# Two gate SiLUs and a root one chunk later on ScalarE, with other first tiles and last tiles, in a two-layer hybrid decoder

## The reference

```python
def reference(x, ...):
    for layer in range(2):
        h = rmsnorm(x, mix_norm_w[layer])
        if layer == 0:  # q, k, v, p from h @ w_in; window attention next to a trailing-mean mixer
            x = x + attn_pool_mixer(h, ...)
        else:           # z, xBC, dt from h @ w_in
            x = x + ssd_mixer(h, ...)
        h = rmsnorm(x, ffn_norm_w[layer])
        x = x + (silu(h @ w_gate) * (h @ w_up)) @ w_down
    return rmsnorm(x, final_norm_w)

def ssd_mixer(u, ...):
    z, xbc, dt_raw = split(u @ w_in)                 # 2048, 3072, 32 columns
    xbc = silu(causal_depthwise_conv(xbc))
    # 32 heads in 4 groups; scan over 8 chunks of 128 tokens
    decay = exp(where(causal, a_cs[l] - a_cs[s], -inf))
    y = (C B^T * decay) @ (x * dt) + C @ state * exp(a_cs) + x * D
    y = y * silu(z)
    y = y * rsqrt(mean over the group's 512 channels of y*y + eps) * norm_w
    return y @ w_out
```

## Time and profile before

| what | value |
|---|---|
| median of three runs | 2259.06 us |
| the profiled execution's own time | 2259.16 us |
| its span | 2257.4 us |
| PE busy | 2245.3 us (99%) |
| POOL, DVE, ACT busy | 1371.0, 1291.7, 1116.1 us |
| chain that ended last | PE 95%, DVE 2%, ACT 1%, issue 1% |
| DMA | 294.06 MB, mean 130 GB/s |

### The profile page before, as it was taken

The page is one execution under the profiler, slowest core; times in us unless marked ns, Lnnn a source line. Parts: engine busy times, 40 slices in busy tenths (PEclk is TensorE's granted clock), DMA queues, the critical chain, the costliest instruction groups (busy, mean ns, idle before and its releaser), DMA issues.

```text
span 2257.4 us, 29178 instructions
## 1 busy us (share of the span) xinstructions
PE 2245.3 (99%) x10646; PEld 1836.0 (81%) x10646; DVE 1291.7 (57%) x1732; ACT 1116.1 (49%) x2044; POOL 1371.0 (61%) x1019
## 2 busy tenths in 40 slices
PE   9999999999999999999999999999999999999998
PEld 7877888888888888888888788888888888888886
DVE  7357663333334898841444579888853243426777
ACT  4046553333333446654455598775643333334445
POOL 3224288777774655687777344343398777764664
PEclk9999999999999999999999999999999999999999
DMA  5110313323226855333332465452233232228744
GB/s 166 47 29 19 119 55 125 122 89 121 89 103 221 291 168 154 122 112 122 103 112 96 153 210 201 141 169 102 86 100 129 89 113 97 103 94 294 243 149 154
DMA packets 169469, 294.06 MB, mean 130 GB/s; under 512 B 19426, under 2 KB 98158, under 8 KB 166767
## 3 DMA queue, kind: packets, MB, share of 16 engines
q1 hardware_dynamic: 165740, 280.26, 36.8%
q10 hardware_dynamic: 3586, 11.93, 1.3%
HBM read 216.00 MB, written 76.15 MB: 129 GB/s over the span
## 4 chain that ended last, share of the span: by engine, by line
PE 95%; DVE 2%; ACT 1%; issue 1%; DMA 0%; POOL 0%; DVEq 0%; ACTq 0%; POOLq 0%
PE ps L2414 51%; PE ps L2118 6%; PE ps L2120 6%; PE ps L2119 6%; PE ps L2500 5%; PE ps L2508 5%; PE ps L2504 5%; PE ps L2856 1%; PE ps L2572 1%; PE ps L2846 1%; PE ps L2839 1%; PE ps L2141 1%; PE ps L2337 1%; PE ps L2370 1%; PE ps L2361 1%
## 5 line engine op out<-in xcount | busy, mean ns | idle before, releaser
L1176 POOL TENSOR_TENSOR s_lo<-s_val,s_hi 128x512 fp32r<-128x512 f32 x154 | 237.2, 1544 | 199.0 <-ACT s_hi L1717 198.3
L3106 DVE TENSOR_TENSOR xres<-ps,xres 128x512 f32<-128x512 f32 x132 | 90.6, 688 | 402.9 <-PE ps L2414 402.9
L1097 POOL TENSOR_TENSOR p_lo<-p_val,p_hi 128x512 fp32r<-128x512 f32 x176 | 238.7, 1366 | 48.5 <-ACT p_hi L1517 37.5
L1517 ACT ACTIVATE p_hi<-p_val 128x512 fp32r<-128x512 f32 x176 | 111.2, 633 | 308.4 <-POOL p_val L1123 308.4
L2414 PE MATMUL ps<-xn_hi,p_hi 128*128 128x512 f32 x704 | 188.8, 390 | 0.0
L2414 PE MATMUL ps<-xn_lo,p_hi 128*128 128x512 f32 x704 | 188.2, 389 | 0.0
L2414 PE MATMUL ps<-xn_hi,p_lo 128*128 128x512 f32 x704 | 188.2, 389 | 0.0
L1717 ACT ACTIVATE s_hi<-s_val 128x512 fp32r<-128x512 f32 x154 | 97.1, 631 | 156.3 <-DMA d_val<-in_w_down 86.6
L2414 PEld LDWEIGHTS ps<-xn_lo,p_hi 128*128 128x128 f32 x704 | 132.2, 188 | 27.5
L2414 PEld LDWEIGHTS ps<-xn_hi,p_lo 128*128 128x128 f32 x704 | 132.2, 188 | 27.5
L2414 PEld LDWEIGHTS ps<-xn_hi,p_hi 128*128 128x128 f32 x704 | 131.7, 188 | 27.1
(11 more groups left out here) (423 smaller groups left out, 5715.4 us busy)
## 6 DMA issues: line engine op xcount, KB each, us to landing
s_val<-hidden SPq DMA_DIRECT2D x154, 256.0 KB, 2.9
hidden<-xres SPq DMA_DIRECT2D x20, 1792.0 KB, 6.5
wv_g<-in_w_gate SPq DMA_DIRECT2D x22, 1024.0 KB, 5.2
wv_u<-in_w_up SPq DMA_DIRECT2D x20, 1024.0 KB, 5.1
d_val<-in_w_down SPq DMA_DIRECT2D x70, 256.0 KB, 3.7
rows_v<-in_w_down SPq DMA_DIRECT2D x64, 256.0 KB, 3.9
mdec<-decay_sums SPq DMA_DIRECT2D x32, 512.0 KB, 4.2
xres<-parked_x SPq DMA_DIRECT2D x24, 512.0 KB, 7.0
```

Of the source, the lines that this page charges most:

```text
L1097: pool.tensor_tensor(p_lo[n][:, :, :], src, f(p_hi[n][:, :, :]), ALU.subtract).then_inc(p_lo_done, 1)
L1176: pool.tensor_tensor(s_lo[i][:, :], s_val[i][:, :], f(s_hi[i][:, :]), ALU.subtract)\
L1517: act.activation(p_hi[n][:, :, :], src, ACT.Copy).then_inc(p_hi_done, 1)
```

## The change

In the scan, three ACT instructions of group 1 (the SiLUs of the last two z halves, and the root of the first sum of squares) are issued behind chunk 1's exponentials instead of behind chunk 0's. `FILL` and PE's order are as before.

```diff
-                    if (g, c) == (1, 0):
+                    if (g, c) == (1, 1):
                         silu_z(ZU - 2)
                         silu_z(ZU - 1)
-                    if g and c == 0:
+                    if g and c == (1 if g == 1 else 0):
                         root(2 * g - 2)
```

```diff
-WARM = (4, 4)
+WARM = 3
...
-                COPIES_AFTER = {3: (0, 1, 2, 3), 7: (4, 5, 6, 7)}
+                COPIES_AFTER = {3: (0, 1, 3), 7: (4, 5, 6, 7)}
...
-            for _ in range(WARM[0]):
-                pe.matmul(ps[:, 5, 0:P], ones_tile[:, :], ones_tile[:, :], start=True, stop=True)
             pe.wait_ge(norm_w_loaded, 16)
             for half in range(2):
-                ins = pe.matmul(norm_w_ps[:, half, :], ones_tile[0:1, :], norm_row[0:1, half * BANK:(half + 1) * BANK],
-                                start=True, stop=True)
-            ins.then_inc(norm_w_loaded, 16)
-            for _ in range(WARM[1]):
+                pe.matmul(norm_w_ps[:, half, :], ones_tile[0:1, :], norm_row[0:1, half * BANK:(half + 1) * BANK],
+                          start=True, stop=True).then_inc(norm_w_loaded, 16)
+            for _ in range(WARM):
...
-            pe.wait_ge(xn_hi_done, NT // 2)
+            pe.wait_ge(xn_hi_done, NT // 2 - 1)
+            pe.wait_ge(part_done, 1)
             column_sums(firsts[0][:, 0, :], Piece(0), 0, 0)
...
+                    if tt:
+                        normed(0, tt, xn_first[tt % 4][:, :], norm_w if tt >= 4 else flat(norm_w_ps)).then_inc(xn_ready, 1)
+                    else:
+                        normed(0, 0, xn_first[0][:, 0:BANK], flat(norm_w_ps), cols=slice(0, BANK))
                         dve.wait_ge(norm_w_loaded, 16 * 3)
-                    normed(0, tt, xn_first[tt % 4][:, :], norm_w if tt >= 4 else flat(norm_w_ps)).then_inc(xn_ready, 1)
+                        dve.scalar_tensor_tensor(xn_first[0][:, BANK:], xres[:, 0, BANK:], rstd[:, 0:1], norm_w_ps[:, 1, :],
+                                                 ALU.mult, ALU.mult).then_inc(xn_ready, 1)
...
                 hi(Piece(0))
+                dve.wait_ge(tail_full, 1)
+                dve.tensor_copy(xn_hi[:, :, 2 * P:3 * P], tail_pair(2).rearrange("p a (b c) -> p (a b) c", c=P))\
+                    .then_inc(part_done, 1)
                 lo(0)
                 lo(1)
```

```diff
+        WEIGHT_SLICES = {SLICES - 9: (4,), SLICES - 8: (5, 6)}
...
+            def weighted(tt):
+                pool.wait_ge(half_ready, tt + 1)
+                pool.wait_ge(norm_w_loaded, 16 * 8)
+                pool.tensor_tensor(xres[:, tt, 0:BANK], xres[:, tt, 0:BANK], norm_wp[:, 0:BANK], ALU.mult)\
+                    .then_inc(last_weighted, 1)
...
+            pool.wait_ge(d_lo_done, 2 * SLICES)
+            weighted(NT - 1)
...
             for tt in range(4, NT):
                 last_square(1, tt)
-                if tt >= 6:
-                    store(tt - 2)
-            act.wait_ge(last_weighted, 1)
-            act.wait_ge(rstd_ready, 5 * NT)
...
+                act.wait_ge(last_weighted, tt - 3)
+                act.wait_ge(rstd_ready, 4 * NT + tt + 1)
+                row = xres[:, tt, 0:BANK]
+                act.activation(row, row, ACT.Copy, scale=rstd[:, tt:tt + 1]).then_inc(last_ready, 1)
+                act.wait_ge(last_ready, tt - 3)
+                act.dma_start(out[0, tt * P:(tt + 1) * P, 0:BANK], row).then_inc(stored, 16)
...
-                        if layer and p >= 7:
-                            final(p - 7)
+                        if layer and p in (6, 7, 9, 10):
+                            final((6, 7, 9, 10).index(p))
...
                     for t_ in range(4):
+                        if t_:
+                            last_reciprocal(3 + t_)
                         add_down("M3", t_, 4, 1)
-                        if t_ >= 1:
-                            final(3 + t_)
-                    final(7)
+                        if t_:
+                            last_scaled(3 + t_)
+                    last_reciprocal(7)
+                    last_scaled(7)
```

More of the change, by code:

```diff
@@ L652, in trunk @@
         pair_full = sem("pair_full")
-        pair_freed, bank_freed = sem("pair_freed"), sem("bank_freed")
+        pair_freed, part_done = sem("pair_freed"), sem("part_done")
         out_full = sem("out_full")
@@ L772, in _ @@
                 if n == 1:
-                    sp.wait_ge(norm_w_loaded, 16 * 2)
+                    sp.wait_ge(norm_w_loaded, 16 * 3)
                     sp.dma_start(norm_w[:, :], mix_norm_w[0].rearrange("(a n) -> a n", a=1).to_broadcast([P, DM]))\
@@ L1036, in _ @@
                 sp.dma_start(out[0, tt * P:(tt + 1) * P, :], xres[:, tt, :]).then_inc(stored, 16)
[L1037 to L1040, removed]
+            for tt in range(4, NT):
+                sp.wait_ge(final_ready, tt + 1)
+                sp.dma_start(out[0, tt * P:(tt + 1) * P, BANK:], xres[:, tt, BANK:]).then_inc(stored, 16)
         @block.gpsimd
@@ L1177, in ffn @@
                         .then_inc(s_lo_done, 1)
+                    if layer:
+                        for tt in WEIGHT_SLICES.get(s, ()):
+                            weighted(tt)
             def q_stage():
@@ L1408, in xhi @@
                     else:
-                        act.wait_ge(tail_full, t.count("tail", 1))
+                        act.wait_ge(tail_full, tt - tail + 1)
                         src = tail_pair(tt)
-                        t.add("tail")
+                        t.n["tail"] = tt - tail + 1
                     act.activation(xn_hi[:, :, tt * P:(tt + 1) * P], src.rearrange("p a (b c) -> p (a b) c", c=P), ACT.Copy)\
@@ L1419, in norm @@
                 t.add("unit", tail)
-                t.add("xhi", NT)
+                t.add("xhi", NT - 1)
             def table(function):
@@ L1743, in ffn @@
                         plain_xhi(p - 7)
-            def store(tt):
-                act.wait_ge(final_ready, tt + 1)
-                act.dma_start(out[0, tt * P:(tt + 1) * P, :], xres[:, tt, :]).then_inc(stored, 16)
             def turn_split(ins, *name):
@@ L2099, in _ @@
                 last_square(1, tt)
-                if tt >= 6:
-                    store(tt - 2)
-            act.wait_ge(last_weighted, 1)
-            act.wait_ge(rstd_ready, 5 * NT)
[L2104 to L2108, removed]
+                act.wait_ge(last_weighted, tt - 3)
[4 more added lines that the diff above has]
+                act.dma_start(out[0, tt * P:(tt + 1) * P, 0:BANK], row).then_inc(stored, 16)
+            act.wait_ge(stored, 16 * (NT + 4))
         @block.tensor
@@ L2224, in project @@
                 if by_bank:
-                    pe.wait_ge(bank_freed, 1)
+                    pe.wait_ge(part_done, 2)
                     p = pair(t.n["unit"])
@@ L2298, in _ @@
                 .then_inc(const_T, 1)
-            pe.wait_ge(xn_hi_done, NT)
+            pe.wait_ge(xn_hi_done, NT - 1)
             column_sums(firsts[0][:, 1, :], Piece(0), 1, 0)
@@ L2931, in normed @@
                 if tt == 0:
[L2932 removed]
+                    dve.wait_ge(norm_w_loaded, 16 * (n_norm + (4 if n_norm else 2)))
                 return dve.scalar_tensor_tensor(dst, xres[:, tt, cols], rstd[:, tt:tt + 1], norm_w[:, cols],
@@ L2944, in make @@
                     if tt == 4:
+                        dve.wait_ge(norm_w_loaded, 16 * 4)
+                    if tt:
+                        normed(0, tt, xn_first[tt % 4][:, :], norm_w if tt >= 4 else flat(norm_w_ps)).then_inc(xn_ready, 1)
+                    else:
+                        normed(0, 0, xn_first[0][:, 0:BANK], flat(norm_w_ps), cols=slice(0, BANK))
                         dve.wait_ge(norm_w_loaded, 16 * 3)
-                    normed(0, tt, xn_first[tt % 4][:, :], norm_w if tt >= 4 else flat(norm_w_ps)).then_inc(xn_ready, 1)
+                        dve.scalar_tensor_tensor(xn_first[0][:, BANK:], xres[:, 0, BANK:], rstd[:, 0:1], norm_w_ps[:, 1, :],
+                                                 ALU.mult, ALU.mult).then_inc(xn_ready, 1)
                 def lo(tt):
-                    dve.wait_ge(xn_hi_done, tt + 1)
+                    if tt == 2:
+                        dve.wait_ge(part_done, 1)
+                    else:
+                        dve.wait_ge(xn_hi_done, tt + (tt < 2))
                     tok = slice(tt * P, (tt + 1) * P)
@@ L3173, in final, with last_reciprocal, last_scaled @@
                 def final(tt):
[L3174 to L3177, removed]
+                    normed(4, tt, xres[:, tt, :], norm_wp).then_inc(final_ready, 1)
+                def last_reciprocal(tt):
+                    dve.wait_ge(std_ready, 4 * NT + tt + 1)
+                    dve.reciprocal(rstd[:, tt:tt + 1], std[:, tt:tt + 1]).then_inc(rstd_ready, 1)
+                def last_scaled(tt):
+                    dve.wait_ge(rstd_ready, 4 * NT + tt + 1)
+                    row = xres[:, tt, BANK:]
```

(4 more changed lines are left out.)

4 lines of the change are left out of this document (removed).

## The result

The changed kernel takes **2267.61 us** (median of 6 runs, 2266.70 to 2268.17). The kernel before took 2259.07 beside it (6 runs, 2258.22 to 2259.96). The ratio is 1.0038, 95% interval 1.0028 to 1.0048: slower by 8.5 us. Forecast were 2266.4, range 2262.8 to 2269.2. The profiled execution took 2268.17 with a span of 2266.4, which is 9.0 more than the span before.

The account below looks back on a forecast made before the run. PE, 99% busy, was taken to bound the kernel. Scan +5.0, clock +1.5, front +0.9 and end -0.1 gave +7.3 on 2259.16, less 0.1 to the median: 2266.4 us, range 2262.8 to 2269.2.

Parts of the forecast that it names:

- The stall: Scan, group 1: PE stands at output part 0 for the first moved SiLU, 5.5 us, bounds 4.6 to 6.0.
- The old wait: Scan, L2856: PE's wait goes because chunk 1 comes earlier on ACT, -0.5 us, with nothing late next.
- The clock: Behind the scan's stall: PE's clock falls from 2.4 to 1.2 GHz, +1.5 us, bounds 0 to +5.3.
- I take 3 us of slow work: Clock term: 3 us of PE work at half clock behind the stall, read from the front's transposes, giving +1.5.
- The front: Kernel start: DVE's added copy of tile 2 makes PE +0.9 us late, bounds -0.9 to +2.2.
- its first part begins about 0.5 earlier: Front: PE's first part starts about 0.5 us earlier, as ACT has three copies instead of four ahead of it.
- The end: Last tiles: PE's wait and store landing shrink, ACT's chain per tile grows; -0.4 to +0.2 us, taken as -0.1.
- the 0.9 wait: Last tiles: PE's 0.9 us wait goes because POOL's weighting of tile 7 no longer meets DVE's last `d_lo`.
- No fall of the clock: First rival, scan: the same stall without the clock falling, +5.8 us in all, 2264.9; chance 35%.
- The long slow stretch: Second rival, scan: clock stays down much longer, up to +5.3 in place of 1.5, 2268.5 and above; chance 7%.
- Better ends: Third rival: stall stands, front -0.5 and end -0.9, no clock fall, +3.6 in all, 2262.7; chance 9%.
- no stall: Fourth rival, scan: PE does not wait at output part 0, +0.3 in all, 2259.4, or 2258 with better front; chance 4%.

Follow-up runs that it names:

- the scan alone: The kernel before with only the scan's edits, both SiLUs and the root behind chunk 1's exponentials: 2265.35 us against 2258.92, ratio 1.0032.
- PE kept busy: The kernel before with the scan's edits plus 25 unused identity matmuls in front of the first output part: 2263.70 us, ratio 1.0022.
- the experiment with the SiLUs back: The changed kernel with the two SiLUs back behind chunk 0, front, end and root as changed: 2259.22 us against 2258.98 for the kernel before.
- The three parts alone: The kernel before with only the scan's, front's or end's edits, each its own kernel: 2265.35, 2259.39 and 2259.30 us.
- the half-filled stall: The kernel before with the scan's edits plus 12 unused identity matmuls in front of the first output part: 2264.01 us against 2259.03, ratio 1.0024.

## Why the prediction was right, and where it was not

The forecast was 1.2 us below the measured time, and the mechanism is the one forecast. By its steps:

**The stall: right.** Forecast 5.5, measured 5.5 in the change and 5.1 in the scan alone, inside the bounds of 4.6 to 6.0. Its parts hold too: ACT waits 1.03 for the load (forecast 0.95) and is through chunk 1 to its last pair in 3.78 (forecast 3.80). No wait of PE on a SiLU stood in the profile before. What gave it away was the rule in `fill_free` and a margin of 0.45 us between the SiLU's end and the matmul. The Trainium skill counts 1.38 us of drain on top of a load ("ScalarE: Activation LUTs", section "What ACT_TABLE_LOAD costs"). Here the load starts at 1354.58 and takes 1.28, and the SiLU starts at 1355.87, so no drain stands behind it. By the page's rule the stall would have been 6.9.

**The old wait: right.** The `mdec` wait of 0.5 is gone, and nothing was late next: 5.5 + 2.8 - 0.5 is the whole shift of 7.8 over the scan.

**The clock: right in kind, too small.** The term of +1.5 measured +2.8 to +2.9 us in the profiled execution of the change and +1.9 in that of the scan alone; with PE kept busy it is nothing. The step that was off is "I take 3 us of slow work": it was 6.0 and 3.9. The slow stretch was 6.8 us long both times, and what differs is how much of it fell on the stall. In the one the clock fell 0.8 before PE came back, in the other 2.9 before. The 3 us came from the front, where the transposes before the rise were counted but not the time at the low clock ahead of them; no run shows that a rise there and a rise behind a stall take the same course. The total came out within 1.2 us because this term was a fifth of it and the rest held. The Trainium skill says in "TensorE: Matmul & The Clock Gate", Part 1, that the throttled clock is the default and activity lifts it. The trace agrees in that 5 us of idleness brought 0.50.

**The front: the sum right, the parts not, so partly luck.** Forecast +0.9, measured +0.97 at the seventh tile. But "its first part begins about 0.5 earlier" failed: it starts at 15.30, before at 15.12. PE opens a PSUM pair for it (`begin_unit`), and lo 0 is what frees that pair; lo 0 now stands behind DVE's copy and runs from 14.03 to 15.2. I had looked at ACT's copies alone. DVE did not gain 0.2 in the norms either: lo 0 is +1.11 late, and 0.15 of that is made up by tile 4.

**The end: the sum right, one reason wrong, so partly luck.** Forecast -0.1, measured -0.1 from the first down matmul to the span's end. ACT's chain takes 2.54 a tile (forecast 2.57), the last issue comes 1.0 later (forecast 0.7 to 1.3), the smaller stores give back 1.1. But the 0.9 wait did not go because POOL's weighting was moved. It hung on the meeting of `s_lo` and the norm, and kernels in which the end was not touched lost it too.

**The rivals.** No fall of the clock (2264.9): against the two slow stretches. The long slow stretch, up to 5.3: what came lies between the forecast's 1.5 and it. Better ends and no stall: the experiment with the SiLUs back and the wait of 5.5 exclude them.

The three parts alone give 6.4 + 0.5 + 0.4 = 7.3, together 8.5. The 1.2 between lies in the scan: its share is 7.8 in the profile of the change and 6.45 in that of the scan alone, 0.35 by a shorter stall and 1.0 by less slow work. Both depend on the execution, and the two slower runs of the scan alone reached +8, so how much of it is chance is not settled.

## What to carry to other kernels

Before moving an instruction behind others, list who waits for it in the code, not in the profile: a wait that is met with 0.45 us to spare stands in no view, and moving the producer by 6 us turned it into the largest wait of the kernel. Move only what the wait asks for, here the root and not the SiLUs. And count a stall like this one, 5 us on TensorE, twice, once as idle time and once as slow matmuls behind it, which the busy share shows as work.

## What the runs showed of the hardware

- In idle stretches the clock fell at different times: 4.7 us after PE's last work in the change, 2.2 in the scan alone, 4.0 at the end of the kernel before. It stayed up through the 1.7 us of the half-filled stall. So a stall of 5.5 or 5.1 us cost 2.9 or 1.9 on top.
- One and the same DMA, chunk 1's load of the decay sums, landed at different times in four profiles, so that ACT stood 1.03, 0.70, 0.78 or 0.12 us for it; the stall was 5.5 with the first of these and would have been 4.6 with the last.
- DVE and POOL excluded each other for a whole instruction in both orders: a norm of 1.28 took 2.39 behind POOL's 1.29, and POOL's `s_lo` took 2.36 behind DVE's norm. The Trainium skill, page "SBUF — State Buffer", section "🔬 SBUF: two separate sides", says that the two share one pair of ports as an exclusive lock that whoever starts first holds. The rows agree that one is held up for the whole of the other. On who is first they agree only where the starts lie 0.08 or more apart; at 0.02 it was the one with the later start, POOL, that held DVE up. So a difference of some 0.1 us decided whether PE stood for 0.9 us at the far end of the chain.
